# Scores two heads at a time, the squares behind the late output projection on ScalarE, and the third weight unit split behind them

## The reference, cut to what matters

```python
h = adaln_pre(x, norm_g[l, 1], mod[:, 1, 0], mod[:, 1, 1])     # rms_norm(x) * (1 + scale) + shift
p = split(h @ w_in[l] + b_in[l])
y_a = nsa_mixer(...)          # 4 query heads of 64; one shared key and value head per branch
y_b = short_conv_mixer(...)
y_c = gated_deltanet(...)     # 4 heads of 64
y_d = mlstm_mixer(...)        # 4 heads of 64
x = x + mod[:, 1, 2] * (concat(rms_norm(y_a), rms_norm(y_b), y_c, y_d) @ w_out[l])
h = adaln_pre(x, norm_g[l, 2], mod[:, 2, 0], mod[:, 2, 1])
x = x + 0.5 * mod[:, 2, 2] * swiglu(h, ffn2_w13[l], ffn2_w2[l])
```

## Time and profile before

| | |
|---|---|
| median of 3 runs | 3679.53 us (3675.2 to 3679.91) |
| the profiled execution | 3665.03 us, of which 3663.3 us span; granted TensorE clock 0.981 of full |
| TensorE matmul busy | 3511.3 us, 96% of the span |
| VectorE, ScalarE, GpSimd busy | 1974.2 us (54%), 1137.5 us (31%), 360.8 us (10%) |
| DMA | 386.35 MB, mean 105 GB/s |

### The profile page before, as it was taken

One profiled execution on the slowest core, in us unless ns is written; L12 is line 12 of the kernel. 1 busy time (PEld: TensorE's weight loads), 2 busy tenths in 40 slices (PEclk: granted clock), 3 DMA queues, 4 the chain that ended last, 5 costly groups with the idle time before them and its releaser, 6 DMA issues.

```text
span 3663.3 us, 45360 instructions
## 1 busy us (share of the span) xinstructions
PE 3511.3 (96%) x16388; PEld 2822.6 (77%) x16388; DVE 1974.2 (54%) x3028; ACT 1137.5 (31%) x1675; POOL 360.8 (10%) x306
## 2 busy tenths in 40 slices
PE   7999999998999999999898899999899999989999
PEld 5888766687888788876678788877678887678887
DVE  6662456556553456344656565445666634656652
ACT  4222334423222222233443222223433313333331
POOL 1000100132000100010013200011110011120002
PEclk9999999999999999999998999999999999999999
DMA  8553222103543355322210154321122332122232
GB/s 320 191 177 103 83 81 70 35 6 106 200 139 104 119 199 186 103 92 70 75 47 5 55 207 166 108 90 64 58 85 93 103 103 77 52 75 91 92 103 86
DMA packets 100377, 386.35 MB, mean 105 GB/s; under 512 B 11086, under 2 KB 12238, under 8 KB 99624
## 3 DMA queue, kind: packets, MB, share of 16 engines
q1 hardware_dynamic: 100264, 384.82, 30.7%
HBM read 382.65 MB, written 2.12 MB: 105 GB/s over the span
## 4 chain that ended last, share of the span: by engine, by line
PE 88%; DVE 5%; ACT 3%; issue 1%; POOL 1%; DMA 1%; SPq 0%; ACTq 0%; DVEq 0%; POOLq 0%
PE bank L2746 19%; PE bank L2748 19%; PE bank L2747 19%; PE bank L2847 4%; PE bank L2849 4%; PE bank L2848 4%; PE bank L2757 1%; PE bank L3136 1%; PE bank L2758 1%; PE bank L2759 1%; PE bank L3132 1%; PE bank L2946 1%; PE bank L3146 1%; ACT wH L1086 1%; PE bank L2930 1%
## 5 line engine op out<-in xcount | busy, mean ns | idle before, releaser
L1086 ACT ACTIVATE wH<-wR 128x1024 fp32r<-128x1024 f32 (+2 forms) x489 | 545.4, 1115 | 1745.5 <-PE bank L2748 1381.0
L1592 DVE TENSOR_TENSOR wL<-wR,wH 128x1024 fp32r<-128x1024 f32 (+2 forms) x489 | 645.8, 1321 | 718.9 <-ACT wH L1086 718.6
L2746 PE MATMUL bank<-hH,wH 128*128 128x512 f32 x2048 | 796.8, 389 | 1.1 <-DVE wL L1592 1.1
L2748 PE MATMUL bank<-hL,wH 128*128 128x512 f32 x2048 | 796.7, 389 | 0.0
L2747 PE MATMUL bank<-hH,wL 128*128 128x512 f32 x2048 | 796.7, 389 | 0.0
L2746 PEld LDWEIGHTS bank<-hH,wH 128*128 128x128 f32 x2048 | 384.4, 188 | 81.1 <-DVE wL L1592 1.5
L2748 PEld LDWEIGHTS bank<-hL,wH 128*128 128x128 f32 x2048 | 384.4, 188 | 80.2
L2747 PEld LDWEIGHTS bank<-hH,wL 128*128 128x128 f32 x2048 | 384.4, 188 | 79.6
L2748 PE MATMUL bank<-gL,wH 128*128 128x512 f32 x1056 | 410.8, 389 | 0.0
L2746 PE MATMUL bank<-gH,wH 128*128 128x512 f32 x1056 | 410.8, 389 | 0.0
L2747 PE MATMUL bank<-gH,wL 128*128 128x512 f32 x1056 | 410.8, 389 | 0.0
(11 more groups left out here) (429 smaller groups left out, 4234.1 us busy)
## 6 DMA issues: line engine op xcount, KB each, us to landing
wR<-in_ffn_w SPq DMA_DIRECT2D x176, 512.0 KB, 3.5
adaw<-in_ada_w SPq DMA_DIRECT2D x144, 512.0 KB, 4.2
wR<-in_ffn_w SPq DMA_DIRECT2D x64, 704.0 KB, 4.0
wR<-in_w_up SPq DMA_DIRECT2D x88, 512.0 KB, 3.5
wR<-in_w_mix SPq DMA_DIRECT2D x76, 512.0 KB, 3.5
wR<-in_w_down SPq DMA_DIRECT2D x32, 704.0 KB, 4.1
wR<-in_w_in SPq DMA_DIRECT2D x40, 512.0 KB, 3.4
wR<-in_w_out SPq DMA_DIRECT2D x16, 512.0 KB, 3.5
```

The lines of the kernel that those rows point to most:

```text
L1086: act.activation(wH[n][:, 0:tiles, :], wR[n][:, 0:tiles, :], ACT.Copy).then_inc(S.w_hi, 1)
L1592: dve.tensor_tensor(wL[n][:, 0:tiles, :], wR[n][:, 0:tiles, :], wH[n][:, 0:tiles, :].bitcast(F32), ALU.subtract).then_inc(S.w_lo, 1)
L2746: pe.matmul(o, wH[n][:, k, :], rH[:, r, :], start=start and k == 0, stop=False)
L2748: mm = pe.matmul(o, wH[n][:, k, :], rL[:, r, :], start=False, stop=stop and k == tiles - 1)
```

## The change

There are three edits, in both layers of the first block only.

1. **Scores in pairs.** TensorE issues the scores of two heads one behind the other, one from partitions 0 to 63, one from 64 to 127, into two banks. In "d" the units are counted anew (`unit_d`): u = 0 and 1 are heads 0 and 1 at j = 0, and so on; TensorE does both at the even u and nothing at the odd one. In "a" it does both at h = 0 and h = 2. It waits until both banks are empty. VectorE takes "a" scores out two at a time, "d" scores one at a time at the old places. `numden` of head 1 moves from unit 11, quarter 3 to unit 10, quarter 2. In `mix_c` both heads of a pair are issued tile by tile.
2. **Squares.** Behind the late output projection ScalarE squares tiles 0 to 6, to `sumsq`, `rstd` and two halves of `hf` by turns (`late_square`); GpSimd adds up five of them (`late_square_sum`); the seventh (`hf[:, 1]`) goes into the mean's matmuls by itself.
3. **Third unit.** At this seam ScalarE does `last_square` ahead of its copy for the third unit, and no table load.

```diff
-    for h, a, b in ((0, (9, 3), (10, 0)), (1, (11, 3), (12, 3)), (2, (15, 3), (16, 3)), (3, (17, 1), (17, 3))):
+    for h, a, b in ((0, (9, 3), (10, 0)), (1, (10, 2), (11, 0)), (2, (15, 3), (16, 3)), (3, (17, 1), (17, 3))):
...
+def unit_d(u):
+    return u // (2 * TT) * 2 + u % 2, u % (2 * TT) // 2
...
-    return 2 * (u + 1) - (u + 1) // TT
+    return sum(2 if unit_d(v)[1] < TT - 1 else 1 for v in range(u + 1))
...
-            def seam_third(u):
-                log_exp()
+            def seam_third(u, load=True):
+                if load:
+                    log_exp()
...
+            def late_square(m):
+                return sumsq[:, :] if m == 0 else hf[:, 1, :] if m == KT - 2 else rstd[:, :] if m % 2 else hf[:, 0, :]
...
             def weights_d(u):
-                h, j = u // TT, u % TT
+                h, j = unit_d(u)
...
             def mix_out():
-                hi(U_UP2, U_UP2 // 2 + 1, KT, 0)
+                for m in range(KT - 1):
+                    if m == TT - 1:
+                        hi(U_UP2, U_UP2 // 2 + 1, KT, 0)
+                    act.wait_ge(S.x_new, at(S.x_new, KT + m + 1))
+                    if 3 <= m < KT - 2:
+                        act.wait_ge(S.pool, at(S.pool, 2 * (2 * KT - 3) + m - 2))
+                    act.activation(late_square(m), xT[:, m, :], ACT.Square).then_inc(S.sq0, 1)
...
-                seam_third(U_UP2 + 2)
...
+                seam_third(U_UP2 + 2, False)
...
             def logits_a(n, h):
...
-                if n < 2 * TT:
+                if n < 2 * TT and h % 2 == 0:
...
-                    dve.wait_ge(S.a_s, at(S.a_s, 4 * n + h + 1))
-                    dve.tensor_tensor_reduce(LL[b][:, h, 0:w], bank[2 + h % 2][:, 0:w], bm[:, h, 384 - P * i:384 - P * i + w],
-                                             1.0, MASKED, ALU.add, ALU.max,
-                                             MX[:, 4 * (b + 1) + h:4 * (b + 1) + h + 1]).then_inc(S.a_l, 1)
-                    if h == H - 1:
+                    for g in (h, h + 1):
+                        dve.wait_ge(S.a_s, at(S.a_s, 4 * n + g + 1))
+                        dve.tensor_tensor_reduce(LL[b][:, g, 0:w], bank[2 + g % 2][:, 0:w], bm[:, g, 384 - P * i:384 - P * i + w],
+                                                 1.0, MASKED, ALU.add, ALU.max,
+                                                 MX[:, 4 * (b + 1) + g:4 * (b + 1) + g + 1]).then_inc(S.a_l, 1)
+                    if h == H - 2:
...
+            def late_square_sum():
+                for m in range(1, KT - 2):
+                    pool.wait_ge(S.sq0, at(S.sq0, KT - 1 + m + 1))
+                    if m > 1:
+                        pool.wait_ge(S.pool, at(S.pool, 2 * (2 * KT - 3) + m - 1))
+                    sq = rstd[:, :] if m % 2 else hf[:, 0, :]
+                    pool.tensor_tensor(sumsq[:, :], sumsq[:, :], sq, ALU.add).then_inc(S.pool, 1)
+                pool.wait_ge(S.pool, at(S.pool, 2 * (2 * KT - 3) + KT - 3))
+                pool.sem_inc(S.sumsq, 1)
...
-                square_sum(KT, 2)
+                late_square_sum()
...
-            def mean_square(n, seam=True):
+            def mean_square(n, seam=True, late=False):
+                if late:
+                    pe.wait_ge(S.sq0, at(S.sq0, 2 * (KT - 1)))
+                    for e, c in enumerate(HALVES):
+                        pe.matmul(bank[MS_BANK[e]][:, 0:W2], ones, hf[:, 1, c], start=True, stop=False)
...
-                    pe.matmul(bank[MS_BANK[e]][:, 0:W2], ones, sumsq[:, c], start=True, stop=False)
+                    pe.matmul(bank[MS_BANK[e]][:, 0:W2], ones, sumsq[:, c], start=not late, stop=False)
...
             def numden(h):
-                pe.wait_ge(S.d_sv, at(S.d_sv, TT * (h + 1)))
+                pe.wait_ge(S.d_sv, at(S.d_sv, 2 * TT * (h // 2 + 1) - 1 + h % 2))
...
             def scores_d(u):
-                h, j = u // TT, u % TT
+                h, j = unit_d(u)
+                if u % 2:
+                    return
...
-                if j == 0 and h % 2 == 0:
+                if j == 0:
...
-                if u >= 2:
-                    pe.wait_ge(S.d_sv, at(S.d_sv, u - 1))
-                pe.matmul(bank[6 + u % 2][:, j * P:], pm[half(h), PD_K + h // 2, j * P:(j + 1) * P],
-                          pm[half(h), PD_Q + h // 2, j * P:], start=True, stop=True).then_inc(S.d_s, 1)
+                if u:
+                    pe.wait_ge(S.d_sv, at(S.d_sv, u))
+                for e in range(2):
+                    pe.matmul(bank[6 + e][:, j * P:], pm[half(e), PD_K + h // 2, j * P:(j + 1) * P],
+                              pm[half(e), PD_Q + h // 2, j * P:], start=True, stop=True).then_inc(S.d_s, 1)
...
-                if n < 2 * TT:
+                if n < 2 * TT and h % 2 == 0:
...
-                    if u >= 2:
-                        pe.wait_ge(S.a_l, at(S.a_l, u - 1))
-                    pe.matmul(bank[2 + h % 2][:, 0:(i + 1) * P], pm[half(h), PA_Q + h // 2, i * P:(i + 1) * P],
-                              pm[half(h), PA_KS + b, 0:(i + 1) * P], start=True, stop=True).then_inc(S.a_s, 1)
+                    else:
+                        pe.wait_ge(S.a_l, at(S.a_l, u))
+                    for e in range(2):
+                        pe.matmul(bank[2 + e][:, 0:(i + 1) * P], pm[half(e), PA_Q + h // 2, i * P:(i + 1) * P],
+                                  pm[half(e), PA_KS + b, 0:(i + 1) * P], start=True, stop=True).then_inc(S.a_s, 1)
...
-                for h in range(H):
-                    if h >= 2:
-                        pe.wait_ge(S.c_v2, at(S.c_v2, n_c_nn(h - 1)))
-                        pe.wait_ge(S.c_v2, at(S.c_v2, n_c_qk(h - 1)))
-                    for b, r, sem in ((4, KBT[h // 2][half(h), :], S.c_kk), (6, pm[half(h), PC_Q + h // 2, :], S.c_kq)):
+                for p in range(2):
+                    for b, r, sem in ((4, KBT[p][:, :], S.c_kk), (6, pm[:, PC_Q + p, :], S.c_kq)):
+                        if p:
+                            pe.wait_ge(S.c_v2, at(S.c_v2, n_c_nn(2) if b == 4 else n_c_qk(2)))
...
-                            mm = pe.matmul(bank[b + h % 2][:, t * P:(t + 1) * P],
-                                           pm[half(h), PC_K + h // 2, t * P:(t + 1) * P], r[:, t * P:(t + 1) * P],
-                                           start=True, stop=True)
-                        mm.then_inc(sem, 1)
+                            for e in range(2):
+                                mm = pe.matmul(bank[b + e][:, t * P:(t + 1) * P],
+                                               pm[half(e), PC_K + p, t * P:(t + 1) * P], r[half(e), t * P:(t + 1) * P],
+                                               start=True, stop=True)
+                                if t == TT - 1:
+                                    mm.then_inc(sem, 1)
...
-                mean_square(2)
+                mean_square(2, late=True)
```

More of the change, by code:

```diff
@@ L283 @@
     "g_lo": 44, "x_new": 24, "ada_in0": 288, "ada_in1": 288, "ada_in2": 288, "ada_in3": 288, "ada_sum": 72,
-    "ada_done": 36, "mod_set": 9, "pool": 39, "sumsq": 3, "ms": 6, "ln": 19, "rstd": 6, "last_sq": 6, "hf": 24,
+    "ada_done": 36, "mod_set": 9, "pool": 31, "sumsq": 3, "ms": 6, "ln": 19, "rstd": 6, "last_sq": 6, "hf": 24,
     "h_hi": 24, "h_lo": 24, "mixc_in0": 16, "mixc_in1": 16, "mixc_in2": 16, "mixc_in3": 16, "pm": 30, "cv": 24,
@@ L294 @@
     "a_ce": 1, "a_ct": 1, "a_ctc": 1, "a_co": 2, "a_s": 32, "a_l": 32, "a_nm": 8, "a_e": 32, "a_t": 32,
-    "a_tc": 32, "a_pv": 32, "a_yv": 20, "y_hi": 8, "y_lo": 8, "x_half": 3, "hf_a": 3, "h_hi_a": 3, "x_part": 8, "o_used": 6}
+    "a_tc": 32, "a_pv": 32, "a_yv": 20, "y_hi": 8, "y_lo": 8, "x_half": 3, "hf_a": 3, "h_hi_a": 3, "x_part": 8, "o_used": 6, "sq0": 7}
 SECOND_COUNTS = {"w_in0": 704, "w_in1": 704, "w_hi": 88, "w_lo": 88, "w_used": 88, "sil": 22, "g_mul": 22, "g_hi": 22,
@@ L750, in build @@
         S.gate_in = sem("gate_in", False)
-        S.sq0 = sem("sq0", False)
+        S.sq0 = sem("sq0")
         S.sq0_used = sem("sq0_used", False)
```

## The result

| | before | changed |
|---|---|---|
| median of the timed runs | 3679.72 us (3675.20 to 3684.38, 4 runs) | 3619.64 us (3614.94 to 3620.92, 4 runs) |
| profiled execution | 3665.03 us | 3618.37 us |
| granted TensorE clock, profiled | 0.981 | 0.985 |

The ratio is 0.9834, 95% interval 0.9817 to 0.9851: 60.1 us faster. The forecast was 3634.4 with a range from 3620 to 3655, so the sign was right and the gain was larger than the range allowed, by a hair. The two profiled executions differ by 46.7 us only, close to the 45.1 of the sum; some of that closeness is luck, since the errors of single terms cancel (last part). The other 13.4 us are the forecast's offset: the profiled execution of before was 14.5 us quicker than its median, that of the changed kernel is 1.3 quicker than its own.

What follows compares the result with a forecast made beforehand. TensorE, busy for 96% of the span, was taken as the bound. 19.6 (squares) + 23.1 ("a") + 4.0 ("d") − 1.6 (mix_c) = 45.1 us, taken from 3679.5: 3634.4 us, eight in ten from 3620 to 3655.

Steps and rivals of the forecast that it cites:

- the forecast's offset: Whole kernel: the median before lay 14.5 us above the profiled execution, and this difference was kept for the changed kernel.
- elsewhere in the mixers TensorE waits most for weights: Mixers: TensorE waits little there, most for weights' low parts, 9.9 us in 12 waits.
- slower, by the clock: Rival, mixers: new short waits bring TensorE's clock to its lower level, 3698 us with 12 slow units; chance 0.04.
- The seams: Behind the late output projection: ScalarE's squares shorten 16.8 us between products to 7.0, gaining 9.8 per layer, 19.6 in all.
- everything behind it is alike ... less some 0.3: Late seam: the FFN seam's 6.15 us plus a 1.2 later start, less 0.3 for other work out of the way: 7.0.
- "a": NSA scores in both layers: paired visits save single scores' time on TensorE, 11.6 us per layer, 23.1 in all.
- the visit behind the wait for `PTR`: "a" at n = 3, h = 1, ahead of the 2.54 us wait for ScalarE's copies: earlier exponentials bring 1.7 us.
- a pair at 1.3 of a single one: Score pairs: a skill-page estimate that would take back 11.6 us, leaving a gain of 33 instead of 45.
- "d": mLSTM scores: 8 paired visits for 16 single ones, gain 2.0 us per layer after losses, 4.0 in all.
- (a): mLSTM units 7, 8, 9 and 11: TensorE waits until VectorE has emptied both banks, costing 2.1 us.
- Its own sign of being wrong: Mixers: the forecast counts as wrong if the clock's row falls below 1.00 there.
- mix_c: mix_c's paired heads: both kinds of scores come later to VectorE, a loss of 0.8 us a layer, −1.6 in all.

Runs made afterwards that it cites:

- second profile of before: The kernel before, unchanged, timed and profiled once more: 3678.0 us median over 12 runs, profiled execution 3680.66 us.
- c_single: The changed kernel with mix_c's scores issued head by head again, as in the kernel before: 3618.03 us.
- before_silu_late: The kernel before with one line moved, silu 0 into unit 27 ahead of quarter 1 instead of the end of unit 26: 3663.75 us, ratio 0.9971.
- third_later: The changed kernel with silu 0 later, odd mLSTM scores' steps earlier, and GpSimd's third-unit low part waiting for VectorE's first normed tile: 3610.7 us, ratio 0.9812.
- after_more_wait: The changed kernel with one more table load written on ScalarE behind silu 0, in both layers: 3618.05 us.

## Why the prediction was right in its mechanism and wrong in its time

**The step that failed** is in the sum: "the median shown is 14.5 above that execution and I let the offset stand". The offset was not the same for both kernels. By the second profile of before it was made of falls of the clock behind the 2.54 us wait of the earlier trace rows, 6.2 us in layer 0 and 6.9 in layer 1, and of 2.8 in mix_c; the change shortens that wait to 1.5 us, and none of the traces with the changed kernel's scores has the long fall until the wait is made longer again. The execution that I read had the wait without the fall, so the rows priced it at 2.5 us. The right reading was at hand: a profile quicker than all three timed runs, and the earlier trace rows showing a long idle of TensorE in the middle of the very place that the change touches. The prediction also says that elsewhere in the mixers TensorE waits most for weights (9.9 us); the same list has 12.7 us for mix_c's `PP`. The rival "slower, by the clock" looked at the clock in the other direction only.

**The seams.** 9.1 us a layer, forecast 9.8. The wait for GpSimd is gone as forecast. The term that was mis-sized is "everything behind it is alike ... less some 0.3": the seam is 1.5 us longer than behind an FFN, not 0.9. ScalarE begins `rstd` 1.2 us later behind the last product than at the FFN's seam (3.40 against 2.24), as the sum has it. VectorE starts on `hf` only 0.3 later (4.36 against 4.07), because at the FFN's seam its weights stand in between; but then `hf` meets GpSimd's low part of the third unit and takes 2.11 us, 1.2 more than there, which the sum left out. The FFN's row:

```profile
413.04 0.87 DVE L1729 SCALAR_TENSOR_TENSOR hf<-xT,modA,rstd 128x256 f32<-128x256 f32 x2
```

Edit 3 by itself brings nothing.

**"a".** 25.3 us, forecast 23.1, without the falls. A single score 512 wide took 1.20 us of TensorE's list, 384 wide 0.98 (distances of products around the visits of both traces), forecast 1.05 and 0.84; the visit behind the wait for `PTR` gave 1.8, forecast 1.7. The remaining 9 us that the "a" pairs gave (34.5 less 25.6) I put down to the falls. That a pair costs what a single score does is shown by the visits' own length, 1.13 us against 1.12, and by the distances between products around the visits at h = 0 and 2, where a pair stands in place of one score: they are the same in both traces within 0.05 us. The estimate made from the Trainium skill's "TensorE: Matmul & The Clock Gate", Part 3, a pair at 1.3 of a single one, is not what this trace shows for two halves.

**"d".** 3.3 us in layer 0, and 3.7 in layer 1 where no fall disturbs it (88.86 in c_single's trace); forecast 2.0. But half of that is the clock. The kernel before has a short fall behind a wait of 2.73 us ahead of unit 19, which the changed kernel's layer 0 doesn't have (window in the first profile, columns as above):

```profile
550.50:553.50 3.00, 3.00 (x8) 2.18 (x7) 1.00 (x2) 1.24 (x2) 0.00 (x0) 0.50 0.00 0
```

The stretch around it is 12.20 us against 10.58. Without it the gain is 1.7 a layer, close to the forecast. All twelve layers of the six traces with the old "d" order have this fall and 6 of the 24 with the new one, at the same wait of 2.7 us; why, no run shows. The waits of (a) are there, 0.45 us each over 8 (3.6 in all), forecast 4.2. In exchange the new order has short falls behind its waits of 2.1 us for weights, in 6 of the 16 layers of the eight traces with the odd steps at quarter 4, of 1.5 to 3.1 us. In the changed kernel's own profile layer 1 gives the gain back (93.56) by falls of both kinds, which the forecast didn't have. Its own sign of being wrong, a clock below 1.00 in the mixers, came up there (0.77), but the kernel before shows it too.

**mix_c.** Forecast −1.6, 0.8 a layer. The wait is there, 3.4 us for `NN`, and pairs cost 0.9 in a layer where the clock falls late, but nothing that the whole stretch or the total shows.

**Adding up.** Seams 18.1, "a" 25.3, "d" 7.0 undisturbed, falls at unit 27 9.6 (before_silu_late's 12.4 less 2.8): 60.0, against 60.1 measured. That the two agree to 0.1 is luck: the 9.6 is uncertain by some 5 either way, and "d" over the sixteen layers of those eight traces is 90.2 us on average against 92.4 over the twelve of the old order, 2.2 a layer and not 3.5. From trace to trace it adds up without medians: the first profile and the changed kernel's are 46.7 apart, of it seams 18.1, "a" 25.3, "d" 2.3, mix_c −0.3, the rest elsewhere; the second profile of before (3680.66) is 62.3 above the changed kernel's, and its falls at unit 27 are 13.0 of that.

## What to carry to other kernels

Before you sum terms against one trace, lay the trace's own time beside the timed runs; where it stands outside them, ask for a second profile of the same kernel and compare start to start, since the offset can sit in the very wait that the change removes. A wait of TensorE of 2.5 us inside a busy stretch is to be priced at its length and at what comes behind it: here some 12 us in the median for one moved line that took 2.8 out of the waits. And where VectorE stands at the end of a seam, look at what GpSimd does at that moment, not only at who is waited for.

## What the runs showed of the hardware

Behind a wait of 2.54 to 2.58 us in an otherwise busy stretch TensorE's granted clock was at its lower level in both layers of three profiled executions, for 13.4 to 16.8 us each, and in neither layer of a fourth, of the same kernel as one of the three; with waits of 2.7 and 3.4 us in the changed kernel it was there for 10.0 and 13.6 us in layer 0 and for 3.2 and 3.4 in layer 1, and with 1.5 us not at all. Behind a wait of 2.7 us ahead of unit 19 it was there for 3.3 to 6.8 us in 12 of 12 layers with the old "d" order and in 6 of 24 with the new one. An operation of VectorE with two inputs in SBUF took 2.30 us instead of 0.48 beside GpSimd's 2.52 (third_later), and two took 2.11 instead of 0.87 beside its 2.94 (the changed kernel). Two float32 scores over 64 partitions each, from the two halves and into two banks, took the time of one: 1.13 us against 1.12. The call for a second table load of the set already loaded left no row in the trace (after_more_wait); whether it was in the program that ran, the trace doesn't tell.
